# Hybrid attention and convolution step on one core: the turn order of an interleaved attention stage, softmax pieces one turn later, keys turned two groups ahead

## What is computed

```python
z = modulate(x, mod[:, 0], mod[:, 1]) @ w_in
h, gb, gc, q, k, v = jnp.split(z, SPLIT_IDX, axis=-1)
y_conv = gb * short_conv(u_ext, conv_w)
# 4 heads, two components of 64 each, values of 128
s = jnp.einsum('bqhcd,bkhcd->bhcqk', q, k) * (QK_HEAD ** -0.5)
p = jax.nn.softmax(jnp.where(mask, s, -jnp.inf), axis=-1)
a = p[:, :, 0] - lam * p[:, :, 1]
o = jnp.einsum('bhqk,bkhd->bqhd', a, v)
# samples: keys and values come from a paged cache
k_past = cache_k[l, page_table].reshape(bs, past, N_HEADS, 2, QK_HEAD)
v_past = cache_v[l, page_table].reshape(bs, past, N_HEADS, V_HEAD)
```

## Time and profile before

| | us |
|---|---|
| median of three runs | 2288.53 |
| the profiled execution | 2287.6 |
| its span, first to last instruction | 2285.7 |
| TensorE busy | 1814.9 (79%) |
| VectorE busy | 1088.3 (48%) |
| ScalarE busy | 515.8 (23%) |
| POOL busy | 317.7 (14%) |

### The profile page before, as it was taken

The page is one execution under the profiler, slowest core; times in us unless marked ns, Lnnn a source line. Parts: engine busy times, 40 slices in busy tenths (PEclk is TensorE's granted clock), DMA queues, the critical chain, the costliest instruction groups (busy, mean ns, idle before and its releaser), DMA issues.

```text
span 2285.7 us, 39884 instructions
## 1 busy us (share of the span) xinstructions
PE 1814.9 (79%) x17492; PEld 1483.2 (65%) x17492; DVE 1088.3 (48%) x1724; ACT 515.8 (23%) x1023; POOL 317.7 (14%) x287
## 2 busy tenths in 40 slices
PE   4799999465766666666665793999999999799992
PEld 1378899344554555545544693777777777799991
DVE  2424121477786776767652567111211111465567
ACT  0301121013223222231231204121112110344441
POOL 0000000122332323323221103400000000000003
PEclk7799999677887788778787797999999999899996
DMA  9711132677998989889876410112112121521112
GB/s 307 273 37 37 37 111 92 226 269 279 415 364 353 364 335 401 324 349 380 329 258 249 157 37 19 56 56 71 58 55 92 55 73 37 221 79 43 43 42 94
DMA packets 133275, 404.29 MB, mean 177 GB/s; under 512 B 12153, under 2 KB 76665, under 8 KB 100338
## 3 DMA queue, kind: packets, MB, share of 16 engines
q0 software_dynamic: 37392, 270.55, 30.4%
q1 hardware_dynamic: 93666, 130.67, 16.9%
q10 hardware_dynamic: 2080, 1.05, 0.2%
HBM read 377.79 MB, written 24.51 MB: 176 GB/s over the span
## 4 chain that ended last, share of the span: by engine, by line
PE 67%; DVE 20%; DMA 8%; issue 2%; ACT 2%; SPq 0%; POOL 0%; DVEq 0%; ACTq 0%; POOLq 0%
PE psum L764 27%; PE psum L1049 11%; PE psum L772 10%; DVE k_ring L1491 5%; DMA k_ring<-cache_k,page_idx 4%; PE psum L877 4%; PE psum L896 3%; DVE p_t L441 3%; DMA ada_w<-w_ada 3%; PE psum L833 3%; PE psum L747 2%; DVE soft L1434 2%; PE psum L842 1%; PE psum L853 1%; DVE x_lo L1332 1%
## 5 line engine op out<-in xcount | busy, mean ns | idle before, releaser
L1491 DVE STREAM_TRANSPOSE k_ring<-k_ring 128x2048 f32<-128x2048 f32 x128 | 294.5, 2303 | 31.1 <-DMA k_ring<-cache_k,page_idx 30.8
L764 PE MATMUL psum<-x_hi,w_hi 128*128 128x512 f32 x896 | 281.6, 396 | 0.0
L764 PE MATMUL psum<-x_lo,w_hi 128*128 128x512 f32 x896 | 277.7, 391 | 0.0
L764 PE MATMUL psum<-x_hi,w_lo 128*128 128x512 f32 x896 | 276.3, 390 | 0.0
L1351 DVE TENSOR_TENSOR w_lo<-w_raw,w_hi 128x2048 fp32r<-128x2048 f32 x37 | 86.9, 2350 | 363.4 <-ACT w_hi L1107 353.8
L1049 PE MATMUL psum<-d_hi,h_hi 128*128 128x256 f32 x704 | 203.2, 289 | 12.7 <-DVE d_lo L1745 12.7
L1049 PE MATMUL psum<-d_lo,h_hi 128*128 128x256 f32 x704 | 200.6, 285 | 0.0
L1049 PE MATMUL psum<-d_hi,h_lo 128*128 128x256 f32 x704 | 200.5, 285 | 0.0
L877 PE MATMUL psum<-k_ring,q_blocks 128*32 128x128 f32 x4096 | 179.8, 331 | 25.3 <-DVE k_ring L1491 24.5
L833 PE MATMUL psum<-k_t,q_zero 128*128 128x512 f32 (+3 forms) x192 | 104.2, 663 | 119.6 <-ACT e_rows L1137 115.6
L764 PEld LDWEIGHTS psum<-x_hi,w_hi 128*128 128x128 f32 x896 | 165.8, 188 | 44.7 <-issue 5.3
(11 more groups left out here) (228 smaller groups left out, 2585.3 us busy)
## 6 DMA issues: line engine op xcount, KB each, us to landing
ada_w<-w_ada SPq DMA_DIRECT2D x12, 2048.0 KB, 9.1
w_raw<-w_in SPq DMA_DIRECT2D x12, 1024.0 KB, 5.3
w_raw<-w_gate SPq DMA_DIRECT2D x11, 1024.0 KB, 5.4
w_raw<-w_up SPq DMA_DIRECT2D x11, 1024.0 KB, 6.2
h_store<-h_out SPq DMA_DIRECT2D x11, 1024.0 KB, 7.8
h_all<-h_store SPq DMA_DIRECT2D x11, 1024.0 KB, 8.9
d_raw<-w_down SPq DMA_DIRECT2D x44, 256.0 KB, 2.9
x_rows<-x_prompt SPq DMA_DIRECT2D x2, 2048.0 KB, 16.7
```

Source lines behind the costliest of these rows:

```text
L764: last = mm(psum[:, 2 * ft + c, 0:CH], w[:, s, k, ft * P:(ft + 1) * P], x[:, k, c * CH:(c + 1) * CH], start=k == 0 and j == 0, stop=k == K ...
L1491: v.transpose(group, group).then_inc(k_turned, 1)
```

## The change

It leaves every computation as it is and moves pieces between turns.

- The rings become `RK` = 5 and `RV` = 3, eight buffers of 1 MB as before. `LAG` becomes 24 and `SLOTS` 155. In GpSimd's list value group m now follows key group m + 26 instead of m + 23.
- TensorE: `turn_max`, `max_to_rows`, `turn_p`, `fold_sums` and `by_query` come one step later. The order inside its turn stays.
- ScalarE: in a turn `keep_p` and `keep_output` come first (two steps later than before), then `keep_turned` or `exps`, then `take_scores`, and `sample_exps` last (two steps later).
- VectorE: in a turn the softmax pieces come first (one step later for `new_scores`, `maximum`, `turn_maxima` and `queries`; two for the others), then the takes and `maxima` or `combine`, and the key turn of group n + 2 comes last. Since a turn that ends with group n + 2 is followed by one that used to begin with that group, the key turns keep their place between the `maxima` of one turn and the softmax pieces of the next; what moves is the takes, from ahead of the key turn to behind it and behind the softmax pieces.

```diff
--- before.py
+++ after.py
@@ -117,12 +117,12 @@
     SCORE_SCALE = QK ** -0.5
     WB = 256
     FT = WB // P
-    GP, RK, RV = 4, 4, 4
+    GP, RK, RV = 4, 5, 3
     STEP = z.PAGES // GP
     REVS = STEP // 4
     NK = z.B * STEP
-    LAG = STEP + 7
-    SLOTS = NK + LAG + 2
+    LAG = STEP + 8
+    SLOTS = NK + LAG + 3
     HEAD0, HEAD_SLOTS = 6, 2 + 4 * z.NT
     NEW0 = z.PAGES * QUAD
     SC = NEW0 + QUAD
@@ -461,13 +461,13 @@
                 pool.indirect_dma_start(to.rearrange("p s d -> p (s d)"), None, rows,
                                         bass.IndirectOffsetOnAxis(page_idx[:, n:n + 1], 0)).then_inc(landed, 16)
 
-            for n in range(NK + LAG):
+            for n in range(NK + LAG + RK - RV):
                 if n < NK:
                     if n >= RK:
                         pool.wait_ge(scored, n - RK + 1)
                     gather(k_pages, k_ring[:, n % RK], k_in[n % RK], n)
-                if n >= LAG:
-                    m = n - LAG
+                if n >= LAG + RK - RV:
+                    m = n - LAG - (RK - RV)
                     if m >= RV:
                         pool.wait_ge(v_used, m - RV + 1)
                     gather(v_pages, v_ring[:, m % RV], v_in[m % RV], m)
@@ -943,15 +943,15 @@
                 if LAG <= n < NK + LAG:
                     value_group(n - LAG)
                 if 1 <= b <= B:
-                    if s == 1:
+                    if s == 2:
                         turn_max(b - 1)
-                    elif s == 2:
+                    elif s == 3:
                         max_to_rows(b - 1)
-                    elif 4 <= s < 4 + REVS:
-                        turn_p(b - 1, s - 4)
-                    if s == 5:
+                    elif 5 <= s < 5 + REVS:
+                        turn_p(b - 1, s - 5)
+                    if s == 6:
                         fold_sums(b - 1)
-                if s == 8 and b >= 2:
+                if s == 9 and b >= 2:
                     by_query(b - 2)
 
             for n in range(SLOTS):
@@ -1170,27 +1170,22 @@
                 act.wait_ge(o_t_done, f + 1)
                 copy(o_t_all[:, f, :], psum[:, MISC, 448:448 + H * S]).then_inc(o_t_kept, 1)
 
-            def slot(n):
+            for n in range(SLOTS):
+                h, u, q = dense_at(n)
                 b, s = n // STEP, n % STEP
+                if 1 <= b <= B and 6 <= s < 6 + REVS:
+                    keep_p(b - 1, s - 6)
+                if s == 10 and b >= 2:
+                    keep_output(b - 2)
+                if u is not None:
+                    if q == 3:
+                        keep_turned(u)
+                    elif q < 2:
+                        exps(u, q)
                 if n < NK:
                     take_scores(n)
-                if 1 <= b <= B:
-                    if s == 2:
-                        sample_exps(b - 1)
-                    elif 4 <= s < 4 + REVS:
-                        keep_p(b - 1, s - 4)
-                if s == 8 and b >= 2:
-                    keep_output(b - 2)
-
-            for n in range(SLOTS):
-                h, u, q = dense_at(n)
-                if q == 3:
-                    keep_turned(u)
-                slot(n)
-                if u is not None and q == 0:
-                    exps(u, 0)
-                elif u is not None and q == 1:
-                    exps(u, 1)
+                if 1 <= b <= B and s == 4:
+                    sample_exps(b - 1)
             stage_end(act, 3)
 
 
@@ -1541,55 +1536,55 @@
                 v.tensor_scalar(o_scaled[:], psum[:, ACC, 0:P], dec[:, 14:15], None, ALU.mult).then_inc(o_scaled_ready, 1)
                 dve.wait_ge(o_scaled_ready, f + 1)
 
-            def slot(n):
-                b, s = n // STEP, n % STEP
-                if n + 1 < NK:
-                    turn_keys(n + 1)
-                if s == 0 and 1 <= b <= B:
-                    maximum(b - 1)
-                if s == 0 and b < B:
+            def softmax_piece(b, s):
+                if s == 1 and b < B:
                     new_scores(b)
-                if b < B:
-                    if s in (4, 8, 12):
-                        turn_maxima(b, s // 4 - 1)
-                    elif s == 10 and b + 1 < B:
-                        queries(b + 1)
                 if 1 <= b <= B:
                     if s == 1:
+                        maximum(b - 1)
+                    elif s == 3:
                         spread_max(b - 1)
-                    elif s == 2:
+                    elif s == 4:
                         negative_max(b - 1)
-                    elif 4 <= s < 4 + REVS:
-                        keep_p(b - 1, s - 4)
-                    if s == 5:
+                    elif 6 <= s < 6 + REVS:
+                        keep_p(b - 1, s - 6)
+                    if s == 7:
                         keep_sums(b - 1)
-                if s == 6:
+                if s == 8:
                     if b >= 2:
                         scale_output(b - 2)
                     if 1 <= b <= B:
                         keep_scale(b - 1)
+                if b < B:
+                    if s in (5, 9, 13):
+                        turn_maxima(b, s // 4 - 1)
+                    elif s == 11 and b + 1 < B:
+                        queries(b + 1)
 
             queries(0)
             turn_keys(0)
+            turn_keys(1)
             for n in range(SLOTS):
                 h, u, q = dense_at(n)
-                if u is None and q == 0:
+                softmax_piece(n // STEP, n % STEP)
+                if n == HEAD0 + H * HEAD_SLOTS:
+                    take_rows(H * NT - 1)
+                elif u is None and q == 0:
                     if h:
                         take_rows(h * NT - 1)
                     take_head_keys(h)
                 elif u is None and q == 1:
                     take_head_queries(h)
-                elif q == 0 and u % NT:
-                    take_rows(u - 1)
-                elif n == HEAD0 + H * HEAD_SLOTS:
-                    take_rows(H * NT - 1)
-                slot(n)
-                if u is not None and q == 0:
+                elif q == 0:
+                    if u % NT:
+                        take_rows(u - 1)
                     maxima(u, 0)
-                elif u is not None and q == 1:
+                elif q == 1:
                     maxima(u, 1)
-                elif u is not None and q == 2:
+                elif q == 2:
                     combine(u)
+                if n + 2 < NK:
+                    turn_keys(n + 2)
             stage_end(dve, 3)
 
 
```

## The result

The changed kernel takes 2190.99 us in the median (2185.38 to 2192.86), the kernel before, measured beside it, 2286.22 us: a ratio of 0.9589 (95% interval 0.9565 to 0.9613), a gain of 94 us by the ratio and 95 by the medians. The forecast was -60 us and 2228 us, its own range 2205 to 2252 and the wide one 2190 to 2272, so the result lies outside the first and 1 us inside the second. The direction and the mechanism were right and the size was too small; the time came out where the second rival, the loads running full, put it (2197 us).

What follows compares the result with a forecast made beforehand. Late consumers, waiting inside four turns, were taken to bound the attention stage, with loads nearly filling the time elsewhere. Long part -59, keys only -2, values only +1 make -60 us: 2228 us, own range 2205 to 2252, wide 2190 to 2272.

Steps and rivals of the forecast that it cites:

- the second rival: Attention stage: the loads run full, all of the long part at 416 to 423 GB/s; -90 us, 2197 us; chance 0.10.
- What bounds the kernel: Attention stage: consumers are late and buffers full in the four turns with `turn_p`; elsewhere loads nearly fill the time.
- Softmax pieces one turn behind, 34.0 to 26 us: Four turns with `turn_p`: `keep_p` finds its data ready, so each stretch takes 8 us less per sequence.
- The takes, counted at nothing by themselves: VectorE: takes behind the key turn save at most 6.9 us of 60.65 in twelve turns, only helping consumers keep up.
- The long part, -59 us: Stretch loading both caches, 612.9 us: consumers and loads meet, loads decide at 396 GB/s, giving 554 us.
- Keys only, -2 us: Start of the attention stage, only keys loading: earlier pieces and takes against one more turn; between -8 and +4 us.
- Values only, +1 us: End of the attention stage: last four turns -8, one more turn +3.8, shorter value ring +5; between -5 and +8 us.
- Ring sizes, charged at nothing: Long part: key loads get four turns to land, value loads three; no cost, since keys come late and values lie ready.
- TensorE's clock: Fewer idle times on TensorE should give some clock back; put at nothing, since TensorE doesn't set the end.
- The signs: Right: `turn_p` waits under 15 us, stretches 25 to 28, long part 385 to 407 GB/s; wrong: TensorE value waits in tens.
- rival 4: Value ring starves TensorE once value loads take over 14.6 us to land; ends slower, near 2330 us; chance 0.06.
- Rivals 1, 3 and 4: 1: waits stay elsewhere, 2269 us (0.17); 3: nothing moves, 2288 us (0.05); 4: value ring starves TensorE (0.06).

Runs made afterwards that it cites:

- half loads: Each page load moves 0.5 MB after the first filling of the rings, compute kept: 2251.11 us in the kernel before, 2117.67 us in the changed kernel.

## Why the prediction was right, and where it was off

- **What bounds the kernel.** Right. Before, loads stopped because the consumers were late (half loads: 90 us for sixteen turns all the same).
- **Softmax pieces one turn behind, 34.0 to 26 us.** Right: 26.5 us, and putting the copies back alone gives 36.9 us and 2277 us. The later steps alone are 71 of 94 us.
- **The takes, counted at nothing by themselves.** Too low: 6 us alone, 11 to 16 us undone. They are part of what the next step missed.
- **The long part, -59 us: the step that was mis-sized.** It put the consumers at 26 + 60.65 us less up to 6.9, 80 to 87 us, let them meet the loads and took 396 GB/s, between two rates of the earlier trace rows. The 60.65 us were no time of the consumers. With half loads the twelve turns take 56.4 us before the change, so 4 us of them were the loads'; 50.6 us with the later steps and ScalarE's order; 47.2 us with the takes behind as well. That makes 72.6 us for sixteen turns and not 80, well below the 82 that the loads need, and the loads then ran without a gap: 410 GB/s, -86 us; 408 to 410 GB/s came in five kernels, with 418 in the fullest stretches. The rate could have been read from the earlier trace rows: the stretch at 407 GB/s had a DMA share of 1.02 and was full, four of the others had shares of 0.92 to 0.98, and the mean of 385 was no rate of the loads. Of the 27 us that the step missed, 19 are the rate (219 MB take 554 us at 396 GB/s, 535 at 410). The other 8 are bytes: the part now has 103 turns and moves 526.7 x 410 = 216 MB, and the sum had left the same 219 MB in it.
- **The page on loads.** The Trainium skill, "DMA: Bandwidth & Descriptors", section "Bandwidth", has 341 GB/s for one load of 1 MB and 435 GB/s for the ports. The prediction let the trace decide against the 341; but the trace has 410 over 527 us of 1 MB loads that overlap in a queue, and doesn't speak of a single load. The ports' figure would have given -109 us in the long part, and the run -86.
- **Keys only, -2 us.** Measured -11, outside its bounds: 24 turns take 3.8 us each for 4.4. This part takes 98.2 us with the copies back in the turn of `turn_p`, 94.6 with ScalarE's old order and 92.9 with the takes ahead, against 90.8. So the first sequence's pieces, counted at 4 us, gave some 7, and ScalarE's order, not counted, some 4, by one profile each.
- **Values only, +1 us.** Measured +0.8, by luck as far as the profiles show: this part took 85.7 to 95.5 us in three kernels with rings of five and three, a spread larger than the term. The third value buffer missing, put at +5 us, is some 15 by the changed kernel's profile (80.3 us with four) and some 8 by the means of these kernels.
- **Ring sizes, charged at nothing.** Right within 10 us. The reason given, that values lie ready, did not last: once the loads set the pace, TensorE waits 108.3 us for them.
- **TensorE's clock.** Its granted clock in the long part rose from 0.81 to 0.88, an average between the levels of 1.2 and 2.4 GHz, while TensorE's busy share there rose from 66% (406.90 of 612.9 us) to 72% (379.61 of 526.7); as foretold it did not set the end. The Trainium skill, "TensorE: Matmul & The Clock Gate", section "What's actually happening", says that activity releases the throttle, and the trace agrees.
- **The signs.** Three of the four for "right" came: 12.5 us of waits for `turn_p`, stretches of 26.5 us, GpSimd's wait down to 250.2. The long part's 410 GB/s and 5.11 us a turn went past the fourth. I had written that waits of TensorE for value data in the tens of us would mean rival 4, and they came to 108.3 us with the time at the range's better end. The sign was badly chosen: once the loads set the pace, somebody has to wait for them, and the ring split decides only who. Landing took 15.7 us at most, over the 14.6 us at which rival 4 was to begin, and the long part shows no cost: 526.7 us, and 532.0 with four value buffers.
- **Rivals 1, 3 and 4** fell: stretches of 26.5 us, loads that stayed full, no slowdown. Rival 2, given 0.10, is what happened, at 410 GB/s for its 416 to 423. That the wide range held is owed to its end having been put at the full rate, and by 1 us to luck: one of the four runs, 2185.38 us, lies outside.

## What to carry to other kernels

Where engines run lists in a fixed order, give every consumer the turn after its producer's, even if it costs a turn of latency: here one wait inside a turn, in thirty-two turns, cost 88 us when it was put back (0.9973 against 0.9589), and moving the steps alone gained 71. To see what such a kernel could gain, take the consumers' pace from a run with the loads made cheap, not from stretches in which both limits are mixed. When a stage has drained one of its rings, let the other stream use it (0.9511 against 0.9589).

## What was not expected of the hardware

Eight buffers of 1 MB are enough to keep the sixteen DMA engines at 410 GB/s over 527 us, though the median load takes 12.6 us from issue to landing and POOL issues each only when a buffer comes free. The time to landing is not fixed for a load here: its median went from 9.7 to 12.6 us with more loads under way, while the rate rose from 358 to 410 GB/s.
